# A two-model transformer kernel: residual kept with features in rows, norms' roots applied after the projections, 512 columns throughout, one unrolled program

## The reference, cut to what matters

```python
def hybrid_layer(h, p_i, ...):                  # first model, per layer
    u = rms_norm(h, norm_g);  z = u @ w_in      # 4096 columns, and 8 for the forget gate
    ...                                         # 8 heads "fox", 8 heads dilated, each gated by silu
    h = h + jnp.concatenate([oa, ob], -1) @ w_out
    gate = jax.nn.sigmoid(rms_norm(h, ple_norm_g) @ w_ple_gate)
    return h + (p_i @ w_ple) * gate

for l in range(DEPTH):                          # second model
    x = x + 0.5 * swiglu(rmsnorm(x, ffn1_norm[l]), ffn1_w1[l], ffn1_w3[l], ffn1_w2[l])
    h = rmsnorm(x, mix_norm[l]);  proj = h @ w_in[l]
    ...                                         # a gated linear recurrence (hgrn2), and a pooling mixer
    x = x + jnp.concatenate([o_a, o_b], -1) @ w_out[l]
    x = x + mem_cross_attention(rmsnorm(x, xa_norm[l]), rmsnorm(mem, mem_norm[l]), ...)
    x = x + 0.5 * swiglu(rmsnorm(x, ffn2_norm[l]), ...)
return rmsnorm(x, final_norm)
```

## Time and profile before

| what | us |
|---|---|
| median of three runs | 3362.6 (3342.3 to 3363.9) |
| the profiled execution, from first to last instruction | 3377.2 |
| TensorE busy in it | 3210.1 |
| VectorE busy | 1494.4 |
| ScalarE busy | 1093.0 |
| mean granted TensorE clock | 0.963 of full |

### The profile page before, as it was taken

How to read it: one execution, slowest core, us unless ns; L and a number is a source line. 1 busy time by engine, 2 the same in 40 slices (tenths; PEclk the granted TensorE clock), 3 DMA queues, 4 the chain that set the end, 5 groups by cost and what they waited for, 6 DMA issues and landing times. The chain is left out here.

```text
span 3377.2 us, 44214 instructions
## 1 busy us (share of the span) xinstructions
PE 3210.1 (95%) x18864; PEld 2834.3 (84%) x18864; DVE 1494.4 (44%) x1752; ACT 1093.0 (32%) x1321; POOL 60.1 (2%) x68
## 2 busy tenths in 40 slices
PE   7999989999979999999999999899999989999998
PEld 7998879898968887988888888788889888888886
DVE  3454443454434445535344444444446353434444
ACT  3433333433332223432333222322225323432222
POOL 0000000000000000010000000000000110000000
PEclk8997998997989999989999999999999999999999
DMA  3111112120222222301322222222223112322222
GB/s 119 64 63 38 59 68 71 39 88 5 71 97 100 97 97 85 120 13 63 105 82 87 89 98 98 77 99 99 87 99 109 42 51 75 107 81 100 90 98 79
DMA packets 41263, 270.99 MB, mean 80 GB/s; under 512 B 6272, under 2 KB 6528, under 8 KB 10016
## 3 DMA queue, kind: packets, MB, share of 16 engines
q1 hardware_dynamic: 41120, 268.99, 22.6%
HBM read 266.81 MB, written 2.10 MB: 80 GB/s over the span
## 5 line engine op out<-in xcount | busy, mean ns | idle before, releaser
L173 DVE TENSOR_TENSOR w_lo<-w_raw,w_hi 128x2048 fp32r<-128x2048 f32 x242 | 554.1, 2290 | 454.1 <-ACT w_hi L167 453.4
L185 PE MATMUL PS<-w_hi,uh 128*128 128x256 f32 x2560 | 734.5, 287 | 12.4 <-DVE ul L329 6.6
L186 PE MATMUL PS<-w_lo,uh 128*128 128x256 f32 x2560 | 727.1, 284 | 0.0
L187 PE MATMUL PS<-w_hi,ul 128*128 128x256 f32 x2560 | 726.9, 284 | 0.0
L167 ACT ACTIVATE w_hi<-w_raw 128x2048 fp32r<-128x2048 f32 x242 | 462.9, 1913 | 637.2 <-PE PS L187 633.3
L185 PE MATMUL PS<-uh,w_hi 128*128 128x512 f32 x1600 | 623.1, 389 | 5.5 <-DVE ul L329 5.5
L186 PE MATMUL PS<-ul,w_hi 128*128 128x512 f32 x1600 | 622.5, 389 | 0.0
L187 PE MATMUL PS<-uh,w_lo 128*128 128x512 f32 x1600 | 622.5, 389 | 0.0
L185 PEld LDWEIGHTS PS<-w_hi,uh 128*128 128x128 f32 x2560 | 494.1, 193 | 24.6 <-issue 15.2
L186 PEld LDWEIGHTS PS<-w_lo,uh 128*128 128x128 f32 x2560 | 494.4, 193 | 1.0 <-issue 1.0
L187 PEld LDWEIGHTS PS<-w_hi,ul 128*128 128x128 f32 x2560 | 494.1, 193 | 0.0
(11 more groups left out here) (280 smaller groups left out, 3219.1 us busy)
## 6 DMA issues: line engine op xcount, KB each, us to landing
w_raw<-in_w SPq DMA_DIRECT2D x242, 1024.0 KB, 4.8
X<-in_x SPq DMA_DIRECT2D x1, 2048.0 KB, 10.1
memory<-in_mem SPq DMA_DIRECT2D x2, 1024.0 KB, 5.0
out<-X SPq DMA_DIRECT2D x4, 512.0 KB, 2.8
bands<-in_bands SPq DMA_DIRECT2D x2, 768.0 KB, 6.0
mask_numbers<-in_masks SPq DMA_DIRECT2D x1, 1152.0 KB, 6.3
p_raw<-in_pT SPq DMA_DIRECT2D x2, 512.0 KB, 6.4
lb<-in_lb_logits SPq DMA_DIRECT2D x2, 512.0 KB, 3.3
```

What stands on the lines that cost most here:

```text
L173: dve.tensor_tensor(self.lo[g % 2][:], self.raw[g % 2][:], self.hi[g % 2][:], ALU.subtract).then_inc(self.lo_done, 1)
L185: pe.matmul(out, sh, mh, start=first, stop=False)
L186: pe.matmul(out, sh, ml, start=False, stop=False)
L187: return pe.matmul(out, sl, mh, start=False, stop=last)
```

## The change

The residual is kept as XT, with features in rows (8 chunks of 128 x 512). A new `Feed` makes the next stage's operand chunk by chunk as soon as a chunk of XT is final: it copies gain times XT as high part (ACT), subtracts for the low part (DVE), squares (ACT) and adds the squares of the chunks (DVE, `total`). No transposes of the residual are left. The transposes of the attention's and the recurrence's outputs stay (`Turn`, four in all). `RowNorm` now gets the mean squares with four matmuls of one column (`sums`), and its root follows later: for outputs with tokens in rows as ScalarE's scale when the result is copied from PSUM, in four instructions of 512 columns where there was one of 2048. For outputs with features in rows it goes as a row R, spread by four transposes (`turn`) and a copy, and multiplied by DVE.

`tokens_block` covers 512 output columns and half of the 1024 features, so that two blocks accumulate into the same PSUM banks: 48 matmuls of 512 columns in a block. The residual projections, the gate and the down blocks now have features in rows. In the feed-forward DVE gets two more instructions of 128 x 1024 a chunk (`scale`, `weigh`), the order becomes up, gate, down of the chunk before, and h's high and low parts have two buffers. In the mixer the query blocks come last, after the pooling's matmuls. The dilated heads' scores take 66 rows as well, two of QT being zero. The memory's norm is made once and without its transposes. All layers are written out as one program of `Stage` objects without barriers. TensorE's program grows from 4,930 rows to 12,146.

```diff
-def block_to_tokens(pe, w, g, u, outs, nt=NT, kd=KD, halves=1, before=None, made=None,
-                    tile_done=None):
...
+def tokens_block(pe, w, g, u, half, outs, nt=NT, ready=None, before=None):
+
+    w.ready(pe, g)
+    order = [(j, t) for j in range(4) for t in range(nt)] if ready else [(j, t) for t in range(nt) for j in range(4)]
+    for j, t in order:
+        k = 4 * half + j
...
+        last = split_products(pe, outs(t), [x[:, k, t * P:(t + 1) * P] for x in u], w.part(g, j * 512, 512), k == 0, k == KD - 1)
...
+    def split_hi(self, act, c):
+        act.wait_ge(*self.x.at(c + 1))
+        act.activation(self.u[0][:, c, :], self.k.XT[:, c, :], ACT.Copy, scale=self.gain(c)).then_inc(self.hi.sem, 1)
...
+        to = self.k.sq[c % 2] if c else self.k.total
+        act.activation(to[:], self.k.XT[:, c, :], ACT.Square).then_inc(self.squared.sem, 1)
...
+    def sums(self, pe):
+        k = self.k
+        pe.wait_ge(*self.feed.summed.at(KD - 1))
+        for t in range(NT):
+            i = pe.matmul(k.PS[:, self.bank, t:t + 1], k.total[:, t * P:(t + 1) * P], k.ones[:, 0:1], start=True, stop=True)
...
+        for t in range(NT):
+            i = pe.transpose(k.PS[:, self.bank, t * P:(t + 1) * P], k.rt[:, t:t + 1].to_broadcast([P, P]), k.ident)
...
         for c in range(1, NCHUNK):
-            order += [up[:, c], down[:, c - 1], gate[:, c]]
+            order += [up[:, c], gate[:, c], down[:, c - 1]]
```

More of the change, by code:

```diff
@@ L655, in _, with project @@
-        project(0, 0)
-        if not dilated:
-            pe.wait_ge(lf_ready, 1)
+                    i = pe.transpose(k.PS[:, pair, t * P:(t + 1) * P], m.zn[j][:, a:a + P], k.ident)
+            i.then_inc(self.turned.sem, 1)
+        def project(part, half, bank, before=None):
+            tokens_block(pe, w, g0 + 2 * part + half, u, half, lambda t: k.PS[:, bank + t, :],
+                         ready=self.u_ready if part == 0 else None, before=before)
+        project(0, 0, 0)
+        if self.rows:
+            self.rows.sums(pe)
@@ new lines, in tensor, with __init__, scalar @@
+        project(2, 0, 4)
+        project(2, 1, 4)
+        pe.wait_ge(*self.even_copied.at(1))
+        pe.wait_ge(*self.odd_copied.at(1))
+        turn(1)
+        pe.wait_ge(*self.v_out.at(1))
+        project(3, 0, 4)
+        for signal, n in self.qk_ready:
+            pe.wait_ge(*signal.at(n))
+        self.scores.products(pe, 0)
+        project(3, 1, 4)
+class HeadsAttention(Stage):
+    def __init__(self, sig, k, m, scores, column, g_out):
+        self.k, self.m, self.scores, self.column, self.g_out = k, m, scores, column, g_out
+        self.pt_act, self.pt_dve, self.out_done, self.mixed = (sig(f"att_{n}", NH) for n in ("ptact", "ptdve", "out", "mixed"))
+    def scalar(self, act):
+        m, turned = self.m, self.scores.turned
@@ new lines, in tensor, with ready, __init__, sync @@
+                    i = pe.matmul(k.PS[:, 6 + f, :], m.Vm[:, j, a:a + P], m.PTm[h % 2][:, j, :], start=j == 0, stop=j == 1)
+                i.then_inc(self.out.sem, 1)
+    def ready(self, pe, c):
+        pe.wait_ge(*self.lo.at(c + 1))
+class Closing(Stage):
+    def __init__(self, sig, k, rows, feed, out):
+        self.k, self.rows, self.feed, self.out = k, rows, feed, out
+        self.done, self.stored = sig("final_done", KD), sig("final_stored", 16 * KD)
+    def sync(self, sp):
+        for c in range(KD):
+            sp.wait_ge(*self.done.at(c + 1))
+            sp.dma_start(self.out[c * P:(c + 1) * P, :], self.k.XT[:, c, :]).then_inc(self.stored.sem, 16)
+        sp.wait_ge(*self.stored.at(16 * KD))
+    def scalar(self, act):
+        self.rows.root(act)
+    def vector(self, dve):
+        k = self.k
+        self.rows.mean(dve)
+        self.rows.refine(dve)
+        dve.wait_ge(*self.rows.turned.at(1))
+        for c in range(KD):
+            dve.scalar_tensor_tensor(k.XT[:, c, :], k.XT[:, c, :], k.final_gain[:, c:c + 1], k.PS[:, self.rows.bank, :],
+                                     ALU.mult, ALU.mult).then_inc(self.done.sem, 1)
+    def tensor(self, pe):
+        self.rows.sums(pe)
+        self.rows.turn(pe)
@@ L1953, in two_models @@
[L1953 to L1961 removed]
+                for s in stages:
+                    s.vector(dve)
```

2530 lines of the change are left out of this document (1296 added, 1234 removed).

## The result

The changed kernel takes 3271.1 us (median of four runs, 3268.2 to 3276.9), the kernel before beside it 3355.4 us (3342.3 to 3363.9): a ratio of 0.974, with a 95% interval of 0.971 to 0.977. It is 2.6% faster, where 5.6% was forecast. The time of 3271 us lies above the range of 3115 to 3250 us. Of the 189 us of the sum, the profiled spans show 110 (3377.2 to 3267.1).

The account below looks back on a forecast made before the run. TensorE's own queue was taken as the bound. Gains of 60 + 121 + 38 less 30 us of costs, 189 us, took the 3377 us span to 3188, less 14.6 a forecast of 3174 us, range 3115 to 3250 us.

Parts of the forecast that it names:

- the sum: Whole kernel: gains of 60, 121 and 38 us less 30 us of costs, 189 us off the profiled span of 3377 us.
- its last step: From span to median: the profiled execution was 14.6 us above the runs' median, so 3188 us became 3174 us.
- three signs of being wrong: Feed-forward chunk over 34 us, dilated stages staying above 60 us, or waits on nothing visible growing with program length.
- 512 columns, 60 us: Token blocks: 227 ns a matmul, 10.9 us a block, saves 60 us; bounds 40 and 65 us.
- Down blocks, 9 us: Feed-forward: TensorE waits for the first addition, losing 0.2 us in each of 44 down blocks; bounds 0 or 62 us.
- The dilated attention, 38 us: Dilated stages: with 66 score rows they run as the fox stages, saving 38 us; lower end 0.
- rival "clock": Dilated attention: its clock still falls to 0.71, giving 3212 us; chance 0.22.
- VectorE holds TensorE: Down blocks and gate: worse order of VectorE's work, 1.4 us lost a down block, giving 3241 us; chance 0.13.
- Boundaries, 121 us: Between stages and at the opening: chunk-by-chunk operands hide most gaps, the gate's only partly; saves 121 us.
- What it adds, 30 us: Costs of sums, turned roots, waits, split copies and down blocks, less 3 us for the memory's norm: 30 us.
- The mixer: Mixer: query blocks last, their scaling ahead of the log gates' low part, costs 3 us a layer, 6 in all.
- The program's length: Rival: some 250 instruction fetches each make TensorE wait, 210 us added, giving 3384 us; chance 0.03.

Follow-up runs that it names:

- Padded: The changed kernel with 128 bytes left free ahead of uh_b, no instruction changed: 3243.6 us, ratio 0.965 to the kernel before.
- ordered: The kernel "Padded" with VectorE's first addition of each down block put ahead of the next low part of weights: 3223.0 us, ratio 0.958.
- Rows64: The changed kernel with 64 rows in the dilated heads' scores and without GpSimd's zeroing of two rows: one run, 3265.0 us.

## Why the prediction was wrong

The direction was right and the size was not. The median lies 97 us above the forecast: 79 from the sum (3188 against a span of 3267), and 18 from its last step. None of the prediction's three signs of being wrong came: a chunk took 33.1 to 33.7 us, the dilated stages 50.7, and the waits did not grow with the program.

**512 columns, 60 us.** Right in its rule: a residual projection went from 46.80 to 43.63 us and a token block to 10.9. By the spacings in the trace the 80 blocks gained some 55 us (929 to 874). The step that failed is "the row of 512 columns shows that the columns set the time then". The row was one of moving operands that suited their weights. The 82 features blocks with u_b pay 6 ns a matmul (232.7 against 226.8 in the mean), 0.28 us a block, 23 us. The sum had no term for it, and no bound.

**Down blocks, 9 us.** The mechanism was right: TensorE waits for the first addition behind the low part of weights, and moving that addition removed the wait. By the starts of its matmuls, each of the changed kernel's down blocks has two spacings of some 0.11 us over the usual, the 0.2 us foretold. But a block grew by 0.4 us, the other half being the difference of 128 in the remainders, 8 us in all. With the 23, tensors' places took 31 us. "Padded" gave back 28 us and "ordered" 20 more, 48 us together.

**The dilated attention, 38 us.** This step failed by its cause: "The change gives it 66. If it then runs as the fox stage". The lower end of 0 and the rival "clock" said how. That rival was the nearest in its cause (3212 us; the 3241 of "VectorE holds TensorE" is nearer in number, for a reason that did not come), and yet not right either, since the dilated stages did speed up and the fox stages slowed down. The four stages gave 11.3 us. But the falls that begin at their ends now run on into the products behind. With these, the time at half clock in and behind the four stages, by the clock's records in the two traces, went from 85.3 only to 75.2 us, and half of the difference, 5 us, is what the clock gave of the 38. Some 33 are missing. Four stages of one execution of one kernel were read as if they showed what 64 and 66 rows do. "Rows64" shows 47.3 and 64.9 us for the same rows. How the last wait bears on a fall at a stage's end is shown (the table above); why the clock falls in one stage and not in another of the same code stays open.

**Boundaries, 121 us.** Right, and a little too low. The gate was to lose 5.5 us at each of two places and 1.3 within; it lost 2.1 (1.0 and 1.1) and nothing, 9 us better in all. The opening's steps came out nearly to the number: first product at 10.8 us (11 foretold), second block at 33.6 (34), end of the forget gate at 62.6 (63).

**What it adds, 30 us.** Four matmuls of the sums took 0.8 us where 0.45 was reckoned, 3 to 4 us in all, and the waits ahead of them were sized well (1.1 to 1.7 us). One edit has no term at all: the zeroing of two rows. It holds up VectorE for 1.6 us at the fox stage's end in each layer, and the fall of the clock behind the longer wait is a part of the 33 us above.

**The mixer.** From the feed-forward's last product to the turn, the kernel gained 9.1 us in layer 0, about as foretold, but 4.5 in layer 1, where a stretch of 13.7 us at half clock is new. Places 31, attention's clock 33, the columns' own shortfall 3, zeroing 3, sums 3 and mixer 7, less the 9 of the boundaries, make 71 of the 79 us, by estimates that are each good to a few us. Some 10 us stay without an owner.

**The last step, 14.6 us.** The profiled execution was taken as a steady 14.6 us above the median. It was an execution with more half-clock time than most: beside the experiments the kernel before ran at 3343 to 3386 us. The changed kernel's profiled execution lies 2 us below its median. Had the spread of the runs been read as that of the clock, the forecast would have been near 3188 and the clock's term smaller.

**Rivals.** VectorE did hold TensorE as far as foretold and no further. The program's length costs nothing that can be seen: 115 packets, and stretches of hundreds of matmuls without a gap.

## What to carry to other kernels

Before a rate read from one stretch is carried to a new layout, look at where the operands lie: here a moving operand should have the same remainder by 256 bytes as the weights beside it, and 128 bytes of padding were worth 28 us of 3271. When TensorE gets faster, look again at what stood just in time behind it. A stage's clock in one profile is a sample: compare two stages only over several executions. Where falls of the clock start at one short wait of a bound TensorE, try throwaway matmuls in it, and price even an instruction on an idle engine (here GpSimd's zeroing) by what runs beside it. And measure a stage from the same instruction to the same instruction in both kernels.

## What the runs showed of the hardware that was not expected

- The spacing of 512-column fp32 matmuls depends on the moving operand's address less the stationary one's, by 256: 227 to 228 ns at 0, 229 at 64, and 232 to 234 at 96, 128, 144, 160, 192 and 224, with no other traffic.
- A zeroing by GpSimd of 2 x 4096 elements (3.5 us) stretched a VectorE instruction of 0.17 us to 1.75 us, until the zeroing ended.
- The same attention stage in one execution ran once at full clock (47.3 us) and once at 0.71 (64.9 us). What decides this is not settled.
- Behind a wait of 2.70 us near a stage's end the clock fell to half for 10 to 17 us in 8 of 8 stages, behind one of 0.97 to 1.12 us in 6 of 24, and with throwaway transposes in the wait in none of 16.
